# A gather stream split between VectorE and TensorE: the split made uneven over time, and the sixteen buffers divided nine and seven

## The reference, cut to what matters

```python
act = gelu(einsum('cd,ced->ce', xc, u[ec]))          # 128 dots with gathered u rows
out = einsum('ce,ced->cd', gate * act, v[ec])        # weighted sum of 128 gathered v rows
```

## Time and profile before

| | |
|---|---|
| median of 3 runs | 2427.22 us (2424.66 to 2429.41) |
| profiled execution | 2433.31 us, span of its trace 2431.6 us |
| TensorE busy | 70% of the span |
| VectorE busy | 65% |
| GpSimd busy | 46% (1,024 indirect DMAs from 863 us to 2403 us) |
| data read from HBM | 755.50 MB |

### The profile page before, as it was taken

The page is one execution under the profiler, slowest core; times in us unless marked ns, Lnnn a source line. Parts: engine busy times, 40 slices in busy tenths (PEclk is TensorE's granted clock), DMA queues, the critical chain, the costliest instruction groups (busy, mean ns, idle before and its releaser), DMA issues.

```text
span 2431.6 us, 23435 instructions
## 1 busy us (share of the span) xinstructions
PE 1712.8 (70%) x7234; PEld 1189.6 (49%) x7234; DVE 1575.7 (65%) x3508; ACT 379.7 (16%) x982; POOL 1118.3 (46%) x1124
## 2 busy tenths in 40 slices
PE   6999968999897803686567566865757776255556
PEld 5887757888684802364227334623624552011112
DVE  3328533630215399868985686798579689977774
ACT  1012511100112102211011221101122111100001
POOL 1001100200000046766775577576557667777774
PEclk9889989999997856799789788978968898678878
DMA  8646535974241578999999999999999999999996
GB/s 283 211 133 223 204 97 171 376 251 152 96 138 44 177 285 307 375 407 409 407 393 395 392 353 404 409 405 354 410 350 382 409 409 374 391 409 409 409 405 258
DMA packets 210158, 757.93 MB, mean 312 GB/s; under 512 B 23036, under 2 KB 26248, under 8 KB 209800
## 3 DMA queue, kind: packets, MB, share of 16 engines
q0 software_dynamic: 161280, 587.27, 62.5%
q1 hardware_dynamic: 48344, 167.35, 19.4%
q10 hardware_dynamic: 432, 2.03, 0.2%
HBM read 755.50 MB, written 1.07 MB: 311 GB/s over the span
## 4 chain that ended last, share of the span: by engine, by line
PE 34%; DVE 29%; POOL 13%; DMA 13%; issue 8%; ACT 2%; POOLq 0%; DVEq 0%; ACTq 0%; SPq 0%
PE psL L452 25%; POOL W L443 13%; DVE W L945 10%; DMA W<-experts_v,crow 7%; DMA W<-experts_u,crow 5%; DVE Z L875 4%; PE psO L452 4%; PE psS L452 2%; PE psT L452 2%; DVE N L875 1%; DVE Sb L875 1%; DVE mx L1022 1%; DMA wring<-weights 1%; DVE Z L881 1%; DVE N L878 1%
## 5 line engine op out<-in xcount | busy, mean ns | idle before, releaser
L452 PE MATMUL psL<-W,con 128*128 128x512 f32 x1024 | 593.0, 718 | 320.6 <-DMA W<-experts_v,crow 277.2
L443 POOL DMA_INDIRECT W<-experts_u,crow x512 | 533.1, 1041 | 562.6 <-DVE crow L878 354.9
L945 DVE SCALAR_TENSOR_TENSOR W<-W,psL 128x1024 f32<-128x1024 f32 x512 | 608.6, 1218 | 186.5 <-DMA W<-experts_u,crow 184.4
L443 POOL DMA_INDIRECT W<-experts_v,crow x512 | 534.2, 1043 | 264.4 <-issue 140.6
L452 PEld LDWEIGHTS psL<-W,con 128*128 128x128 f32 x1024 | 211.9, 225 | 652.7 <-issue 534.8
L452 PE MATMUL psL<-N,wring 128*128 128x256 f32 x1744 | 398.9, 390 | 22.5 <-DVE N L875 12.5
L452 PEld LDWEIGHTS psL<-N,wring 128*128 128x128 f32 x1744 | 337.7, 195 | 76.7 <-issue 11.4
L875 DVE SCALAR_TENSOR_TENSOR Z<-W,crow,Z 128x1024 f32<-128x1024 f32 x252 | 323.4, 1283 | 52.6 <-DMA W<-experts_v,crow 46.9
L427 POOL DMA_DIRECT2D W<-ada x96 | 50.9, 530 | 456.9 <-DVE W L1075 456.1
L1495 ACT ACTIVATE con<-con,crow 128x128 f32<-128x128 f32 x256 | 98.0, 396 | 569.6 <-PE psL L452 321.9
L452 PE MATMUL psO<-N,wring 128*128 128x128 f32 x928 | 125.4, 292 | 60.9 <-DVE N L878 50.5
(11 more groups left out here) (213 smaller groups left out, 1555.1 us busy)
## 6 DMA issues: line engine op xcount, KB each, us to landing
wring<-weights SPq DMA_DIRECT2D x311, 512.0 KB, 5.4
W<-ada POOLq DMA_DIRECT2D x96, 512.0 KB, 5.6
W<-experts_u,crow POOLq DMA_INDIRECT x512, 6.7
W<-experts_v,crow POOLq DMA_INDIRECT x512, 6.7
W<-rel_rows SPq DMA_DIRECT2D x1, 1536.0 KB, 8.9
X<-x_dram ACTq DMA_DIRECT2D x1, 1024.0 KB, 6.1
out<-N SPq DMA_DIRECT2D x1, 1024.0 KB, 3.9
W<-rel_rows SPq DMA_DIRECT2D x1, 768.0 KB, 4.9
```

Of the source, the lines that this page charges most:

```text
L443: pool.indirect_dma_start(W[:, slot * D:(slot + 1) * D], None, experts_u if kind == "u" else experts_v, bass.IndirectOffsetOnAxis(ap=idx[: ...
L452: return pe.matmul(o, l, r, start=first, stop=last)
L945: dve.scalar_tensor_tensor(out=row, in0=row, scalar=1.0, in1=hps, op0=ALU.mult, op1=ALU.mult, accum_out=dots[:, col:col + 1]).then_inc(row ...
```

## The change

Which engine consumes a v row now depends on the tile and the place. In the stretches `PE_MORE` (tile 0: places 32 to 111; tiles 1 and 2: 64 to 127 and 152 to 223) TensorE takes three of four v rows, elsewhere in tiles 0 to 2 one of four. Tile 3 keeps one of two. VectorE's share of the sixteen slots falls to nine in tiles 0 to 2, and TensorE's rises to seven; tile 3 keeps eleven and five. A slot is now the least recently filled one of the engine's range, and the waits follow from lists worked out beforehand. `BEHIND` falls from 6 to 4.

```diff
-def on_pe(i):
-    return i % 2 == 0
-RING = {"dve": 11, "pe": 5}
-BASE = {"dve": 0, "pe": 11}
+PE_MORE = [((32, 112),), ((64, 128), (152, 224)), ((64, 128), (152, 224)), ()]
+
+def on_pe(t, i):
+    if t == 3:
+        return i % 2 == 0
+    place = PLACE.index(("v", i))
+    return i % 4 != 3 if any(a <= place < b for a, b in PE_MORE[t]) else i % 4 == 0
+
+DVE_SLOTS = [9, 9, 9, 11]
+FREED, SLOT, BEFORE, LANDED, PE_ROWS = [], [], [], [], []
...
+    _slot = min(range(_dve_slots) if _who == "dve" else range(_dve_slots, GRING),
+                key=lambda s: (-1 if _taken[s] is None else _taken[s], s))
+    SLOT.append(_slot)
+    BEFORE.append(None if _taken[_slot] is None else FREED[_taken[_slot]])
...
-BEHIND = 6
+BEHIND = 4
...
-                if count > RING[who]:
-                    pool.wait_ge(row_pe if who == "pe" else row_dve, count - RING[who])
+                if BEFORE[n] is not None:
+                    who, count = BEFORE[n]
+                    pool.wait_ge(row_pe if who == "pe" else row_dve, count)
...
-                    first, last = count % V_PE == 1, count % V_PE == 0
+                    first, last = count == (PE_ROWS[t - 1] if t else 0) + 1, count == PE_ROWS[t]
...
-                dve.wait_ge(row_pe, (t + 1) * V_PE)
+                dve.wait_ge(row_pe, PE_ROWS[t])
```

More of the change, by code:

```diff
@@ L95 @@
         PLACE.append(("v", _q // 2) if _q % 2 else ("u", LEAD + _q // 2))
-def on_pe(i):
-    return i % 2 == 0
-RING = {"dve": 11, "pe": 5}
-BASE = {"dve": 0, "pe": 11}
-FREED = []
-_dve = _pe = 0
+PE_MORE = [((32, 112),), ((64, 128), (152, 224)), ((64, 128), (152, 224)), ()]
[6 more added lines that the diff above has]
+FREED, SLOT, BEFORE, LANDED, PE_ROWS = [], [], [], [], []
+_rows = {"dve": 0, "pe": 0}
+_taken, _uses = [None] * GRING, [0] * GRING
 for _n in range(4 * PER):
     _kind, _i = PLACE[_n % PER]
[L110 to L116, removed]
+    _who = "pe" if _kind == "v" and on_pe(_n // PER, _i) else "dve"
+    _rows[_who] += 1
+    FREED.append((_who, _rows[_who]))
+    _dve_slots = DVE_SLOTS[_n // PER]
+    _slot = min(range(_dve_slots) if _who == "dve" else range(_dve_slots, GRING),
+                key=lambda s: (-1 if _taken[s] is None else _taken[s], s))
+    SLOT.append(_slot)
+    BEFORE.append(None if _taken[_slot] is None else FREED[_taken[_slot]])
+    _taken[_slot] = _n
+    _uses[_slot] += 1
+    LANDED.append(16 * _uses[_slot])
+    if _n % PER == PER - 1:
+        PE_ROWS.append(_rows["pe"])
 AHEAD = 6
-BEHIND = 6
+BEHIND = 4
 V_AT = {_i: _p for _p, (_kind, _i) in enumerate(PLACE) if _kind == "v"}
[L125 to L132, removed]
 def build(nc, x_dram, c_row, ada, weights, small, vecs, cons, experts_u, experts_v, out):
@@ L438, in _ @@
                     pool.wait_ge(idx_ready, 2 * t + 1 + i // (SLOTS // 2))
-                who, count = FREED[n]
-                if count > RING[who]:
-                    pool.wait_ge(row_pe if who == "pe" else row_dve, count - RING[who])
-                slot, at = slot_of(n), t % NT * SLOTS + i
+                if BEFORE[n] is not None:
+                    who, count = BEFORE[n]
+                    pool.wait_ge(row_pe if who == "pe" else row_dve, count)
+                slot, at = SLOT[n], t % NT * SLOTS + i
                 pool.indirect_dma_start(
@@ L470, in rows @@
                         continue
-                    slot = slot_of(t * PER + p)
-                    first, last = count % V_PE == 1, count % V_PE == 0
+                    slot = SLOT[t * PER + p]
+                    first, last = count == (PE_ROWS[t - 1] if t else 0) + 1, count == PE_ROWS[t]
                     if first and t:
@@ L475, in rows @@
                     pe.wait_ge(diag_ready, count)
-                    pe.wait_ge(row_landed[slot], landing(t * PER + p))
+                    pe.wait_ge(row_landed[slot], LANDED[t * PER + p])
                     for b in range(2):
@@ L926, in rows @@
                         who, count = FREED[t * PER + p]
-                        slot, col = slot_of(t * PER + p), T * SLOTS + i
+                        slot, col = SLOT[t * PER + p], T * SLOTS + i
                         row = W[:, slot * D:(slot + 1) * D]
@@ L940, in rows @@
                             continue
-                        dve.wait_ge(row_landed[slot], landing(t * PER + p))
+                        dve.wait_ge(row_landed[slot], LANDED[t * PER + p])
                         if kind == "u":
```

## The result

The changed kernel takes 2435.74 us in the median (2435.07 to 2436.27, 6 runs) against 2428.41 us for the kernel before (2424.66 to 2433.47, 6 runs): a ratio of 1.0026, with a 95% interval of 1.0015 to 1.0037, or 7.3 us more. The profiled execution took 2435.89 us, with a span of 2434.2 us. The profiled execution of before was among its slower runs (2433.31 us), so the two traces differ by only 2.6 us of span where the medians differ by 7.3. Stage by stage they can be compared; their sums are about 5 us too kind to the new kernel.

What follows compares the result with a forecast made beforehand. Transfers bind most of the second half; in the attention GpSimd's descriptor work, held up by VectorE's v rows, falls behind. Terms -14.4 + 10 + 5.4 + 5.0 = +6.0 us on 2427.22 gave 2433 us, range 2414 to 2449.

Steps and rivals of the forecast that it cites:

- The attention is bound by GpSimd's issues, stretched by VectorE's v rows: Attention, tiles 0 to 2: fewer v rows on VectorE relieve GpSimd; -18.0 + 3.6 = -14.4 us.
- half of the excess: Attention: POOL's excess busy time, 10.7, 11.0 and 5.9 us, was to halve, a gain of 13.8 us.
- The 4.2 us of waiting for TensorE's rows: Start of two attention stages: GpSimd's wait for a TensorE row goes with seven slots and BEHIND 4, a gain of 4.2 us.
- The 3.6 us for the residual of tile 0: Tile 0's residual: two more TensorE rows lengthen the projection that VectorE waits for, a loss of 3.6 us.
- Tile 0's search, 10 us for VectorE's extra rows: Search beside tile 0: 24.1 us of extra VectorE rows, four fifths of 17.7 us idle usable, a loss of 10 us.
- the three rounds: Tile 0, places 112 to 135: one more VectorE row each, 3.6 us, hidden in 25.4 us of idle time.
- The searches and heads, 5.4 + 5.0 us: Tiles 1 and 2: searches lose 5.4 us to VectorE's rows (bound +11 each), heads 5.0 to two fewer slots.
- The signs named ahead: Profile after: attention issues toward 1.04 us, over 380 GB/s; tile 0's search below 400; head waits at places 9 and 17.
- the sign of being wrong: Places 32 to 63: the forecast would be wrong if GpSimd waits for VectorE there with the queues empty.
- A: Rival, 2419 us, chance 0.30: VectorE's extra rows absorbed in searches and heads; needs losses outside the attention under 9.5 us.
- B: Rival, 2430.5 us, chance 0.20: only the count of stretched issues matters, 264 v rows instead of 256, 3.3 us.
- C: Rival, 2448 us, chance 0.12: third TensorE row and ScalarE's later exp outlast GpSimd's pace; sign: 10.2 us job grows 1 us.

Runs made afterwards that it cites:

- e4b: Kernel before, with VectorE's v rows up to place 221 adding the token row in PSUM instead of the SBUF accumulator: 2409.69 us against 2429.36, ratio 0.9919.
- e7c: Changed kernel with three of four v rows on TensorE only beside the attention, one of two elsewhere; nine/seven slots there, eleven/five elsewhere: 2416.58 us, ratio 0.9933 against before.
- e3b: Changed kernel with three of four v rows on TensorE only beside the attention, one of two elsewhere; nine and seven slots kept: 2431.74 us against 2429.36, ratio 1.0011.
- e2b: Changed kernel's split and BEHIND 4 with the old eleven and five slots, at slow transfers: 2620.23 us against 2533.7 for the kernel before, ratio 1.0333.
- e7b: The same kernel as e7c, run at slow transfers: 2519.93 us against 2512.03 for the kernel before, ratio 1.0036.

## Why the prediction was right, and where its terms weren't

The forecast was +6 us, 2433, and the measured difference is +7.3, at 2435.74 us inside the range. The mechanism held in outline: the attention gains by relief of GpSimd, and the places outside it lose more than that. That the sum came within 1.3 us is luck. The gain was forecast at 14.4 us and the traces have 25.7; the losses were forecast at 20.4 and the traces have 29.5, with the trace of before some 5 us too long for its median. Two errors of opposite sign made up for each other.

*The attention is bound by GpSimd's issues, stretched by VectorE's v rows: right, and shown (e4b).* Its size was too small, 14.4 us net against 25.7 in the traces. I took half of the excess because half of the v rows go. The excess of POOL's busy time went from 10.7, 11.0 and 5.9 us to 59.29 - 61 x 0.94 = 2.0, 56.44 - 57 x 0.94 = 2.9 and 51.65 - 54 x 0.94 = 0.9, by four fifths, 21.8 us. The 4.2 us of waiting for TensorE's rows at the start of two attentions went as forecast (0.45 us are left, in tile 2), and the two together are 26.0.

Why four fifths and not half can be counted. In the three windows VectorE began 43 v rows before and 22 after, so the number did halve. Under 40 of the 43 and 19 of the 22 an issue began and was stretched. But it began on average 0.44 us into the v row before and 0.78 us after, and since it ends at about 2.09 us after the v row's start either way, it is stretched less the later it begins. Two of the changed kernel, beside tile 0:

```profile
962.71 1.28 DVE L880 SCALAR_TENSOR_TENSOR Z<-W,crow,Z 128x1024 f32<-128x1024 f32 x1
...
971.61 1.28 DVE L880 SCALAR_TENSOR_TENSOR Z<-W,crow,Z 128x1024 f32<-128x1024 f32 x1
```

```profile
963.23 1.57 POOL L448 DMA_INDIRECT W<-experts_u,crow  x1 [0.30 <-issue]
...
972.56 1.14 POOL L448 DMA_INDIRECT W<-experts_v,crow  x1 [0.30 <-issue]
```

963.23 + 1.57 = 964.80 = 962.71 + 2.09, and 972.56 + 1.14 = 973.70 = 971.61 + 2.09. The halving could be forecast; the later start is a matter of how the two engines fall into step, and why it moved isn't shown.

The 3.6 us for the residual of tile 0 aren't seen, but 10.3 us are lost between places 112 and 128, right behind the dense stretch.

*Tile 0's search, 10 us for VectorE's extra rows: the size of the loss in tile 0 was right (11.5), its place and so its cause not.* From place 168 to the end of the tile GpSimd loses nothing (+3.2 to +1.8), though VectorE is as full as forecast. Most had gone by place 128, where I had costed the three rounds at nothing, behind 25.4 us of VectorE's idle time. Three traces tell what it is. From place 96 to the end of tile 0, e7c (eleven slots, one v row of two, 14.7 places of lookahead) loses nothing (-9.1 to -9.6). e3b (nine slots, one of two, 12 places) loses 4.1 us (-8.6 to -4.5). The change (nine slots and, from place 112, three of four, 10.3 places) loses 10.8 (-9.0 to +1.8). So the fewer slots cost some 4 us and VectorE's extra rows some 7 more. The rows did cost, as the forecast had it, but at VectorE's pauses in the residual and not in the full search; whether by their own time or by the shorter lookahead that they bring, these runs don't divide. VectorE's idle time didn't cover it.

*The searches and heads, 5.4 + 5.0 us: 18.0 were lost (20.0 at the heads, less 2.0 won ahead of them).* This is the term most mis-sized. It is two terms, and e3b, with the nine slots of the change but one v row of two at the tile's end, divides them. Its heads lose 2.8, 1.8 and 0.4 us, 5.0 in all: the 5.0 that I had for the slots. Its wait at place 9 of tile 2 ends 9.6 us before that of the change:

```profile
1672.20 0.94 POOL L448 DMA_INDIRECT W<-experts_u,crow  x1 [4.73 <-DVE W L950]
```

The other 15 us of the change's heads go with VectorE's extra v rows, in places 224 to 255 and 32 to 63. Less the 2.0 won ahead of them, 13 us stand against the 5.4 of the sum, and within the upper bound of 11 for each tile. Of the 8.3 us that VectorE saves in places 168 to 223, the issues gain 3.2 and 4.0 us from place 168 to 224; the rows added behind make the first u row of tile 2 come at 1680.3 instead of 1675.6 us. Even tile 3, which keeps eleven slots, loses 6.7 us at its head, where e3b loses 0.4.

*The signs named ahead.* POOL's mean issue in the attentions fell below the 1.04 us forecast, to 0.97, 0.99 and 0.96, with 392, 400 and 387 GB/s. Tile 0's search fell to 389 and 382 GB/s, and the waits at the heads of tiles 1 and 2 are at places 9 and 17. In places 32 to 63 of tiles 1 and 2 GpSimd does wait for VectorE, up to 4.20 us at once, as it did before (up to 4.18), but with the DMA at 409 GB/s, so the sign of being wrong isn't met.

*The rivals.* A (faster) fell: losses outside the attention were far over its 9.5 us. B (the count of v rows decides) fell in its mechanism: POOL's busy time over the 1542 us from 863 to 2405 fell from 1067.2 to 1041.9 us, though VectorE has eight v rows more. The rule of the Trainium skill that stands beside it ("SBUF — State Buffer", "Who interferes with whom") agrees with e4b as to which operand interferes; how much it costs went here with the number of v rows and with the moment at which the issue begins. C (TensorE becomes the bound of the attention) fell, narrowly:

```profile
1836.00 0.66 PE L573 MATMUL psT<-con,Pb 128*128 128x128 f32 x4 [0.76 <-DVE Pb L883]
...
1838.65 5.32 PE L457 MATMUL psL<-W,con 128*128 128x512 f32 x12
1844.90 0.65 PE L573 MATMUL psT<-con,Pb 128*128 128x128 f32 x4 [0.93 <-DVE Pb L883]
```

Three rows end at 1844.0, and TensorE still waits 0.93 us for VectorE's maps, where it waited 2.26 to 2.41. The sign given for C was a job 1 us longer than 10.2 us; this one takes 1844.90 - 1836.00 = 8.9. The granted clock of that stage is 0.95 where it was 0.85, with 5.32 / 3 = 1.77 us a row instead of 1.80 and 0.65 us for the transposes instead of 0.83, so the margin may owe something to it.

How much of the 7.3 us is slots and how much VectorE's rows can be bounded only. e3b has the slots of the change and one of two rows outside the attention; it stands at 1.0011 against 1.0026, 3.6 us apart with intervals that overlap, and 6.4 us apart in the traces. Giving e3b its slots back is worth 19 us. With the attention's gain the terms are then of the size of 20 us each for gain and lost lookahead, and a few us for the rows. The slots alone on the old split, and the new split on the old slots, weren't measured at full transfer rate. Nor was `BEHIND` = 4 by itself; since e7c has it too, it isn't what costs.

## What to carry to other kernels

When a stream of transfers runs through a fixed number of buffers, count the lookahead in places, slots divided by the consumer's share of the rows, stretch by stretch, and set it against the pauses of that consumer; here its idle time didn't say what a shorter lookahead would cost. The same better split in the attention was worth 15 us once the buffers were divided stage by stage as well (e7c), and nothing, 2.4 us slower, when one division had to serve all (e3b). And look at the engine that issues: its busy time over its count of issues showed a bound that neither VectorE's share nor the DMA's did.

## What the runs showed of the hardware beyond that

An indirect DMA of 128 rows of 4 KB costs GpSimd 0.94 us and 0.30 us until the next. A v row of VectorE with both tensor inputs in SBUF, 1.28 us long, stretches an issue that begins under it so that it ends about 2.09 us after the v row's start, to 1.94 us where it begins 0.15 us in. It leaves an issue that began before it alone, and with one input in PSUM it stretches none (e4b). Where such v rows follow one another without a gap, at 1.37 us each, most issues are stretched only to 1.10 us or less.

With slow transfers (in e2b, mostly in tile 3, 178 issues in 260 us, 1.46 us each, against 1.28) every variant lost to the kernel before, even e4, whose edit only takes an SBUF input from VectorE's v rows (1.016):

```profile
2200.00:2460.00 260.00, 109.45 (x154) 35.93 (x152) 195.29 (x297) 18.00 (x46) 180.03 (x178) 0.67 0.93 356
```

One chip had both, 2429 us beside e4b and 2512 beside e7b, so the cause needn't be a lasting property of a chip. It stays open, as does what makes e4 slower there; the kernel before has no trace with such transfers.
